# Operand layout and access order in the large fp32r matmuls of a two-block layer on one core

## The reference

```
h  = rmsnorm(concat(meta, x)) @ w_in          # 2048 x 10240, 272 rows
x  = x + merged(h) @ w_out
h  = rms_norm(x) @ w_in_2                     # retention, gated delta rule, gates
x  = x + merged2(h) @ w_out_2
x  = x + cross_attention(rms_norm(x) @ w_xq, rms_norm(mem) @ w_xkv) @ w_xo
x  = x + square(relu(rms_norm(x) @ w_ff1)) @ w_ff2
out = rms_norm(x)
```

## Time and profile before

| | |
|---|---|
| median of 3 runs | 2828.58 us |
| the profiled execution | 2828.21 us |
| its span, first to last instruction | 2826.5 us |
| TensorE matmul busy | 2808.4 us (99%) |
| TensorE weight load busy | 2442.2 us (86%) |
| VectorE busy | 1931.8 us (68%) |
| ScalarE busy | 1351.7 us (48%) |
| HBM traffic over the span | 178 GB/s |

### The profile page before, as it was taken

The page is one execution under the profiler, slowest core; times in us unless marked ns, Lnnn a source line. Parts: engine busy times, 40 slices in busy tenths (PEclk is TensorE's granted clock), DMA queues, the critical chain, the costliest instruction groups (busy, mean ns, idle before and its releaser), DMA issues.

```text
span 2826.5 us, 38749 instructions
## 1 busy us (share of the span) xinstructions
PE 2808.4 (99%) x15872; PEld 2442.2 (86%) x15872; DVE 1931.8 (68%) x2513; ACT 1351.7 (48%) x1726; POOL 59.2 (2%) x102
## 2 busy tenths in 40 slices
PE   9999999999999999999999999999999999999998
PEld 8899888888888888888888888888888888888887
DVE  7645567778766658898988875556666656666556
ACT  5434654347334436555555543444345434444434
POOL 0000210000000000000000000000000000000000
PEclk9999999999999999999999999999999999999999
DMA  7444344565555544434343445544354454554453
GB/s 278 179 188 156 145 173 182 189 235 192 201 182 190 185 178 170 145 139 149 135 149 135 159 170 196 200 185 161 139 199 188 179 208 182 205 200 188 185 203 149
DMA packets 72849, 506.66 MB, mean 179 GB/s; under 512 B 8384, under 2 KB 8512, under 8 KB 12896
## 3 DMA queue, kind: packets, MB, share of 16 engines
q1 hardware_dynamic: 71136, 497.83, 47.6%
q0 software_dynamic: 1104, 5.90, 0.6%
q10 hardware_dynamic: 432, 0.45, 0.0%
HBM read 499.95 MB, written 2.10 MB: 178 GB/s over the span
## 4 chain that ended last, share of the span: by engine, by line
PE 92%; DVE 5%; ACT 1%; issue 1%; DMA 1%; SPq 0%; POOL 0%; DVEq 0%; ACTq 0%
PE double L1376 85%; PE bank L1376 6%; DVE wlo L2079 1%; DVE cacc L2085 1%; PE bank L1379 1%; DVE cst L2102 0%; ACT whi L1737 0%; DVE AA L2085 0%; DVE cst L2079 0%; DMA vec<-in_vec 0%; DVE cacc L2082 0%; DVE Cm L2079 0%; DVE Tn L2593 0%; DMA raw<-in_wall 0%; DVE acc L2079 0%
## 5 line engine op out<-in xcount | busy, mean ns | idle before, releaser
L1376 PE MATMUL double<-AA,whi 128*128 128x512 f32 (+1 forms) x5008 | 1641.8, 380 | 2.8 <-DVE wlo L2079 2.8
L1737 ACT ACTIVATE whi<-raw 128x1024 fp32r<-128x1024 f32 x926 | 925.4, 1049 | 819.9 <-PE double L1376 780.7
L1376 PE MATMUL double<-AA,wlo 128*128 128x256 f32 (+1 forms) x4624 | 1296.4, 280 | 0.0
L2079 DVE TENSOR_TENSOR wlo<-raw,whi 128x1024 fp32r<-128x1024 f32 (+1 forms) x934 | 1101.1, 1214 | 195.0 <-ACT whi L1737 192.4
L1376 PEld LDWEIGHTS double<-AA,whi 128*128 128x128 f32 x5008 | 915.2, 188 | 180.5 <-DVE wlo L2079 4.6
L1376 PEld LDWEIGHTS double<-AA,wlo 128*128 128x128 f32 x4624 | 874.0, 189 | 1.4
L1376 PE MATMUL double<-whi,AA 128*128 128x512 f32 x1536 | 482.7, 389 | 0.7 <-DVE wlo L2079 0.7
L1376 PEld LDWEIGHTS double<-whi,AA 128*128 128x128 f32 x1536 | 288.5, 188 | 56.4 <-DVE wlo L2079 1.1
L1376 PE MATMUL double<-whi,BB 128*128 128x512 f32 x1024 | 309.1, 381 | 0.0
L1376 PE MATMUL double<-wlo,AA 128*128 128x512 f32 x768 | 296.5, 386 | 0.0
L1376 PEld LDWEIGHTS double<-whi,BB 128*128 128x128 f32 x1024 | 191.9, 187 | 33.7
(11 more groups left out here) (338 smaller groups left out, 1721.6 us busy)
## 6 DMA issues: line engine op xcount, KB each, us to landing
raw<-in_wall SPq DMA_DIRECT2D x462, 1024.0 KB, 4.8
raw<-in_wall SPq DMA_DIRECT2D x9, 256.0 KB, 6.4
X<-in_xT SPq DMA_DIRECT2D x1, 2048.0 KB, 11.3
Mm<-in_memT POOLq DMA_DIRECT2D x1, 2048.0 KB, 15.4
tmp<-rqk POOLq DMA_DIRECT2D x16, 128.0 KB, 2.2
mblk<-in_memT SPq DMA_DIRECT2D x8, 256.0 KB, 3.3
dec<-in_dec POOLq DMA_DIRECT2D x1, 1536.0 KB, 8.6
hs<-in_hsT SPq DMA_DIRECT2D x4, 272.0 KB, 5.6
```

The costliest lines, as they stand in the source:

```text
L1376: return q.matmul(out, lhsT, rhs, start=start, stop=stop, skip_group_check=True)
L1737: q.activation(hi_of(j)[:, c], raw[j % RAW][:, c], ACT.Copy).then_inc(S("w_hi"), 1)
L2079: return q.tensor_tensor(out, a, b, o)
```

## The change: what it does

The high and the low part of one k-tile now lie side by side: `AA` is seen as `[16, 2, 272]` (`AL`) or `[16, 2, 256]` (`AT`), `BB` as `[8, 2, 256]`. With the 256-wide layout `both` is one contiguous run of 512 columns. Kind T matmuls whose tag is not in `META_TAGS` walk moving operand and output by `leap` (4 rounds of runs of 8 with a step of 32, as kind N), over 512 columns and over 256; those in `META_TAGS` keep the plain order. `whi` and `wlo` have 32 and 48 spare columns, and `hi_of` and `lo_of` choose an offset so that every set begins at byte 128 of 256. The ScalarE and VectorE steps that write the parts follow the layout: those that wrote 512 contiguous columns (`A2`, `b_hi`, `b_lo`) write two runs of 256 with a gap of 256.

```diff
+META_TAGS = ("gp", "q", "mp", "ga", "ma")
...
-    whi = [ar.get([P_, UNIT + 0], F32R, f"whi{i}") for i in range(SPL)]
-    wlo = [ar.get([P_, UNIT + 64], F32R, f"wlo{i}") for i in range(SPL)]
+    whi_at = [ar.off + 4 * (UNIT + 32) * i for i in range(SPL)]
+    wlo_at = [ar.off + 4 * (UNIT + 32) * SPL + 4 * (UNIT + 48) * i for i in range(SPL)]
+    whi = [ar.get([P_, UNIT + 32], F32R, f"whi{i}") for i in range(SPL)]
+    wlo = [ar.get([P_, UNIT + 48], F32R, f"wlo{i}") for i in range(SPL)]
...
-    AA = ar.get([P_, 2, NT * L], F32R, "AA")
-    Ahi, Alo = AA[:, 0, :], AA[:, 1, :]
+    AA = ar.get([P_, 2 * NT * L], F32R, "AA")
+    AL = AA[:, :].rearrange("p (k s n) -> p k s n", s=2, n=L)
+    AT = AA[:, 0:2 * NT * T].rearrange("p (k s n) -> p k s n", s=2, n=T)
...
-    BB = ar.get([P_, 2, 8 * T], F32R, "BB")
+    BB = ar.get([P_, 8, 2, T], F32R, "BB")
...
     def A2(t, j):
-        return t[:, 2 * j * T:2 * (j + 1) * T]
+        return AT[:, 2 * j:2 * j + 2, t, :]
...
-        return (0, 16 if pr["kind"] == "T" else 0)
+        return (128, 128) if kind == "T" else (128, 128)
...
-        o = set_off(j)[0]
+        o = (set_off(j)[0] - whi_at[j % SPL]) % 256 // 4
...
-        o = set_off(j)[1]
+        o = (set_off(j)[1] - wlo_at[j % SPL]) % 256 // 4
...
             if pr["ready"][0] == "b_lo":
-                return BB[:, :, a * T:(a + 1) * T]
+                return BB[:, a, :, :]
             if pr["kind"] == "W":
-                o, n = a * L, L
-            elif pr["tag"] in ("gp", "q", "mp", "ga", "ma"):
-                o, n = a * L + META, T
-            else:
-                o, n = a * T, T
-            return AA[:, :, o:o + n]
-
-        def leap(x):
-            return x.rearrange("p (b s r) -> p s b r", s=4, r=8)
+                return AL[:, a, :, :]
+            if pr["tag"] in META_TAGS:
+                return AL[:, a, :, META:L]
+            return AT[:, a, :, :]
+
+        def leap(x, s=4, r=8):
+            return x.rearrange("p (b s r) -> p s b r", s=s, r=r)
...
-                        mm_group(out[0:n, m * 512:m * 512 + 2 * T], wh[:, i, c], both, start=first, stop=False)
-                        ins = mm_group(out[0:n, m * 512:m * 512 + T], wl[:, i, c], hh, start=False, stop=last)
+                        o, h = out[0:n, m * 512:m * 512 + 2 * T], out[0:n, m * 512:m * 512 + T]
+                        if pr["tag"] in META_TAGS:
+                            mm_group(o, wh[:, i, c], both, start=first, stop=False)
+                            ins = mm_group(h, wl[:, i, c], hh, start=False, stop=last)
+                        else:
+                            mm_group(leap(o, 4, 8), wh[:, i, c], leap(flat(both), 4, 8), start=first, stop=False)
+                            ins = mm_group(leap(h, 4, 8), wl[:, i, c], leap(hh, 4, 8), start=False, stop=last)
...
         def b_hi(i, r):
-            q.activation(flat(Bhi[:, 2 * i:2 * i + 2, :]), tmps[r["t"]][:, :], ACT.Copy).then_inc(S("b_hi"), 1)
+            q.activation(BB[:, 2 * i:2 * i + 2, 0, :], two(tmps[r["t"]][:, :]), ACT.Copy).then_inc(S("b_hi"), 1)
```

More of the change, by code:

```diff
@@ L1155, in program @@
     boff = ar.off
-    BB = ar.get([P_, 2, 8 * T], F32R, "BB")
-    Bhi = BB[:, 0, :].rearrange("p (a b) -> p a b", a=8)
-    Blo = BB[:, 1, :].rearrange("p (a b) -> p a b", a=8)
+    BB = ar.get([P_, 8, 2, T], F32R, "BB")
     q0 = ar.off
@@ L1337, in set_off @@
     def set_off(j):
-        pr = P.pairs[units[j][0]]
-        return (0, 16 if pr["kind"] == "T" else 0)
+        kind = P.pairs[units[j][0]]["kind"]
+        return (128, 128) if kind == "T" else (128, 128)
     def hi_of(j):
-        o = set_off(j)[0]
+        o = (set_off(j)[0] - whi_at[j % SPL]) % 256 // 4
         return whi[j % SPL][:, o:o + UNIT]
     def lo_of(j):
-        o = set_off(j)[1]
+        o = (set_off(j)[1] - wlo_at[j % SPL]) % 256 // 4
         return wlo[j % SPL][:, o:o + UNIT]
@@ L1761, in s_a1 @@
                 q.wait_ge(S(f"hs{HS[k]}"), 16)
-            q.activation(Ahi[:, k * L:(k + 1) * L], hs[:, k, :], ACT.Copy, scale=V("norm_gain", k)).then_inc(S("a_hi"), 1)
+            q.activation(AL[:, k, 0, :], hs[:, k, :], ACT.Copy, scale=V("norm_gain", k)).then_inc(S("a_hi"), 1)
         def s_sq0(j, r):
@@ L1827, in s_a2 @@
             q.wait_ge(S("merged"), at["au", k]["m"])
-            q.activation(A2(Ahi, k), flat(Macc[:, 2 * k:2 * k + 2, :]), ACT.Copy).then_inc(S("a_hi"), 1)
+            q.activation(A2(0, k), Macc[:, 2 * k:2 * k + 2, :], ACT.Copy).then_inc(S("a_hi"), 1)
         def s_nrm(key, r):
@@ L1877, in f @@
                 q.wait_ge(S("ev"), at["res", (r["res"], k // 2)]["ev"])
-                q.activation(Ahi[:, k * T:(k + 1) * T], X[:, k, :], ACT.Copy, scale=scale(k)).then_inc(S("a_hi"), 1)
+                q.activation(AT[:, k, 0, :], X[:, k, :], ACT.Copy, scale=scale(k)).then_inc(S("a_hi"), 1)
             return f
@@ L1980, in s_memn @@
             q.wait_ge(S("w_used"), r["used"])
-            q.activation(Ahi[:, k * T:(k + 1) * T], mblk[k // 2][:, k % 2 * T:(k % 2 + 1) * T], ACT.Copy,
+            q.activation(AT[:, k, 0, :], mblk[k // 2][:, k % 2 * T:(k % 2 + 1) * T], ACT.Copy,
                          scale=V("norm_mem_g_2", k)).then_inc(S("a_hi"), 1)
@@ L1998, in s_a4 @@
             q.wait_ge(S("w_used"), r["used"])
-            q.activation(A2(Ahi, j), flat(Macc2[:, 2 * j:2 * j + 2, :]), ACT.Copy).then_inc(S("a_hi"), 1)
+            q.activation(A2(0, j), Macc2[:, 2 * j:2 * j + 2, :], ACT.Copy).then_inc(S("a_hi"), 1)
         def s_x_s(h, r):
@@ L2011, in s_a6 @@
             q.wait_ge(S("xat_vec"), at["x_o", (j // 2, j % 2)]["o"])
-            q.activation(A2(Ahi, j), flat(Mx[:, 2 * j:2 * j + 2, :]), ACT.Copy).then_inc(S("a_hi"), 1)
+            q.activation(A2(0, j), Mx[:, 2 * j:2 * j + 2, :], ACT.Copy).then_inc(S("a_hi"), 1)
         def s_f1(i, r):
@@ L2118, in s_a1 @@
             q.wait_ge(S("a_hi"), r["hi"])
-            c = slice(k * L, (k + 1) * L)
-            stt(Alo[:, c], hs[:, k, :], V("norm_gain", k), Ahi[:, c].bitcast(F32), ALU.mult, ALU.subtract).then_inc(S("a_lo"), 1)
+            stt(AL[:, k, 1, :], hs[:, k, :], V("norm_gain", k), AL[:, k, 0, :].bitcast(F32), ALU.mult, ALU.subtract).then_inc(S("a_lo"), 1)
         def s_sq0(j, r):
@@ L2183, in b_lo @@
             q.wait_ge(S("b_hi"), r["hi"])
-            hi = flat(Bhi[:, 2 * i:2 * i + 2, :]).bitcast(F32)
-            tt(flat(Blo[:, 2 * i:2 * i + 2, :]), tmps[r["t"]][:, :], hi, ALU.subtract).then_inc(S("b_lo"), 1)
+            hi = BB[:, 2 * i:2 * i + 2, 0, :].bitcast(F32)
+            tt(BB[:, 2 * i:2 * i + 2, 1, :], two(tmps[r["t"]][:, :]), hi, ALU.subtract).then_inc(S("b_lo"), 1)
         def s_mix(g, r):
@@ L2278, in f @@
                 q.wait_ge(S("a_hi"), r["hi"])
-                tt(A2(Alo, j), src(j), A2(Ahi, j).bitcast(F32), ALU.subtract).then_inc(S("a_lo"), 1)
+                tt(A2(1, j), src(j), A2(0, j).bitcast(F32), ALU.subtract).then_inc(S("a_lo"), 1)
             return f
@@ L2284, in f @@
                 q.wait_ge(S("a_hi"), r["hi"])
-                c = slice(k * T, (k + 1) * T)
-                stt(Alo[:, c], X[:, k, :], gain(k), Ahi[:, c].bitcast(F32), ALU.mult, ALU.subtract).then_inc(S("a_lo"), 1)
+                stt(AT[:, k, 1, :], X[:, k, :], gain(k), AT[:, k, 0, :].bitcast(F32), ALU.mult, ALU.subtract).then_inc(S("a_lo"), 1)
             return f
@@ L2690, in s_memn @@
             q.wait_ge(S("a_hi"), r["hi"])
-            c = slice(k * T, (k + 1) * T)
-            stt(Alo[:, c], mblk[k // 2][:, k % 2 * T:(k % 2 + 1) * T], V("norm_mem_g_2", k), Ahi[:, c].bitcast(F32),
+            stt(AT[:, k, 1, :], mblk[k // 2][:, k % 2 * T:(k % 2 + 1) * T], V("norm_mem_g_2", k), AT[:, k, 0, :].bitcast(F32),
                 ALU.mult, ALU.subtract).then_inc(S("a_lo"), 1)
@@ L2799, in vector_program @@
                "k": s_k, "v": s_v, "vtr": s_vtr, "att_z": s_att_z, "att_o": s_att_o, "mp": gate_in(rx), "ma": gate_in(rx), "pu": s_pu,
-               "ga": s_ga, "au": s_au, "a2": split_low(lambda j: flat(Macc[:, 2 * j:2 * j + 2, :])),
+               "ga": s_ga, "au": s_au, "a2": split_low(lambda j: Macc[:, 2 * j:2 * j + 2, :]),
                "a3": gained_low(lambda k: g12[:, k:k + 1]), "a5": gained_low(lambda k: V("norm_x_g_2", k)),
-               "a7": gained_low(lambda k: V("norm_ffn_g_2", k)), "a4": split_low(lambda j: flat(Macc2[:, 2 * j:2 * j + 2, :])),
-               "a6": split_low(lambda j: flat(Mx[:, 2 * j:2 * j + 2, :])), "begin2": s_begin2, "res": s_res, "nrm": s_nrm,
+               "a7": gained_low(lambda k: V("norm_ffn_g_2", k)), "a4": split_low(lambda j: Macc2[:, 2 * j:2 * j + 2, :]),
+               "a6": split_low(lambda j: Mx[:, 2 * j:2 * j + 2, :]), "begin2": s_begin2, "res": s_res, "nrm": s_nrm,
                "fold": s_fold, "fin": s_fin, "mixs": s_mixs, "mixf": s_mixf, "xn": s_xn, "trig": s_trig, "gab": s_gab, "gab1": s_gab1,
```

## The result

The changed kernel takes 2835.13 us (median of 12 runs, 2834.31 to 2836.98) against 2828.65 us: a ratio of 1.0023 with a 95% interval of 1.0015 to 1.0031. It is 6.5 us slower, where 39 us less were forecast. The profiled execution has a span of 2833.3 us.

The account below looks back on a forecast made before the run. TensorE's matmul rate was taken as the bound. Kind T gains of 29.4 us (undisturbed stages) and 9.5 us (stages cut by side groups), other terms 0, gave 2828.2 - 38.9 = 2789 us; range 2763 to 2829.

Parts of the forecast that it names:

- What bounds the kernel: Whole kernel: TensorE matmuls busy 2808.4 of 2826.5 us, never kept waiting; the rate at which matmuls follow each other decides.
- the 10 that were named as the limit: Sign in the profile after: TensorE's waits should stay under 10 us in all.
- The 512 of a pair has f2's form ... I take 220 ns.: Kind T's 512-column matmul in runs of eight: from about 230 to 220 ns, bounds 220 and 230.
- The 256 measured 113, as taken: Kind T's 256-column matmul in runs of eight: 113 ns, half way between 109 and 117, because its load nearly fills it.
- Side groups leave the two streams in a new position ... I take half: pu, rq, rk, dq, dk, dv, xq, cut by side groups: half the gain, 1,408 pairs x 6.75 = 9.5 us.
- mk was counted as undisturbed: mk listed with au, wo, wo2, xo, f1 as uncut stages: 2,176 pairs at full gain, 29.4 us.
- mv and f2 are good already: Kind N stages mv and f2: already at the fast rate, no change counted.
- dealt anew: Kind N in rv, rg, gta, gz, gtb: states redistributed; all good gains 10.6 us, all bad costs as much; taken 0.
- I take 0: Changed start bytes in 896 plain pairs (-3 or +7 us) and kind W (2 us either way): 0 for both.
- no change (1): Rival: kind T stays at 230 + 117; time 2828, or 2825 to 2835 with the plain pairs; chance 0.11.
- The limit of 0.2%: Whole kernel time: within 0.2% (5.7 us) no measurement of this kernel can tell a change.
- Rival 4: Kind T slower: the 256 in runs of eight makes load and stream meet, pair about 358 ns, 2867 us; chance 0.12.

Follow-up runs that it names:

- Run 11: Changed kernel, but the second matmul of a kind T pair also moves all 512 columns, in the same runs; 3204.14 us, one run.
- run 4: Changed kernel, but only the 512-column matmul of a kind T pair in runs of eight, the 256 in plain order; 2846.64 us, ratio 1.0063.
- run 10: run 9's kernel, but kind T's 256-column matmul walked in two rounds of 128 columns (step 16) instead of four of 64; 2821.32 us, 0.9975.
- run 6: Kernel before the change, with only kind T's low weights moved from byte 192 to byte 128; 2851.97 us, ratio 1.0085.
- run 9: Changed kernel, but the kind T unit right before each kind N stage in plain order with low weights at byte 192; 2812.52 us, ratio 0.9944.
- run 5: Changed kernel, but kind T's low weights begin at byte 192 as in the kernel before; 2837.48 us, ratio 1.0044.

## Why the prediction was wrong

**What bounds the kernel** held: 99% busy, no wait of weight (11.6 us in all, a little over the 10 that were named as the limit), all in the rate at which matmuls follow each other; and that the run order has two rates, 220 and 231.

**"The 512 of a pair has f2's form ... I take 220 ns."** This term was mis-sized: it measured 227 (226 to 227). The form of a matmul is not enough, its neighbours belong to it. Run 11 shows 220 in f1 for the same operands with a second 512, run 4 shows 230 beside a plain 256. The 256 measured 113, as taken; that the weight load sets it was not tested. The pair is 340 and not 333, the term 22 us and not 39.

**"Side groups leave the two streams in a new position ... I take half"** was wrong for kind T, in the change's favour: after a side group the pairs of dk, dq and dv come back to 227 + 113 (means 226.9 and 114.3 against 226.7 and 113.5 in f1). In the changed kernel the pair has one steady rhythm, where kind N has two. With other edits the pair has more than one as well: in run 10 it took 341 in f1 and 352 in wo. And mk was counted as undisturbed, though 124 side matmuls cut into its stage; at half the gain that would have been 1.7 us less.

**"mv and f2 are good already"** is the step that failed, and it decided the sign. I saw that the rate of kind N is inherited, and applied that to the retention stages ("dealt anew"), with 10.6 us either way. I did not apply it to mv and f2, which ran at 220 throughout, though each follows a kind T stage that the change alters. They measured 230.6. Their 220 was a product of the old handover (runs 6 and 9); 20 us hung on it. With it in the range, 2829 would have been 2849.

**"I take 0" for the start bytes** was right for plain pairs and kind W (1.3 us together), and wrong in what it looked at: the byte of kind T's low weights was priced in the matmuls that read it, and it acts on f2, which doesn't read it (run 6). On those that read it, it acts as well once they go in runs: 340 a pair at byte 128, 350 at byte 192 (run 5).

**The rivals**: no change (1) reaches up to 2835 and so has the measured time, by luck: its mechanism, a kind T that gains nothing, is refuted by the 340. The range, which ended at 2829, left that upper part out without a reason. The limit of 0.2% below which no change could be told was too wide as well: the interval of the result is 1.0015 to 1.0031. Rival 4, slower by a bad 256, is refuted: the 256 gained. The rule of the Trainium skill in PSUM — Partial Sum Buffer, section Specifications (TRN2), that non-contiguous patterns slow matmuls, is contradicted for 256 columns too: 113 in runs of eight, 117 plain. The rule of the Trainium skill in SBUF — State Buffer, section Who interferes with whom, that TensorE never waits on anyone, is about one engine holding up another. It neither explains nor rules out what is seen here, the same f2 at 220 or at 230.6, since no run shows what f2 waits for; rival 1 read more out of it than it says.

**What stays open**: what the streams meet in. That it is their relative timing is an inference from two rates of one instruction stream; no run shows the collision itself. Nor is it known why mv and f2 took different rates in runs 5, 6 and 11, after kind T with the same bytes, or why the first f2 of run 4 differs from the others. Byte 192 with plain order gave 220 in both every time it was run; byte 128 mostly gave 230.6 or more, not always.

## What to carry to other kernels

A matmul rate that takes two values for one form belongs to the sequence, not to the instruction: before changing what stands ahead of a stage at the better rate, ask what put it there, and put its loss into the range. When a gain at one place and a loss at another come from the same constant, set it by place: here a single plain unit with another start byte before each stage turned 6.5 us lost into 16 us gained. And a form tested in one neighbourhood (512 after 512) is a bound for another (512 beside 256), not its price.

## What the runs showed of the hardware

With a mean granted clock of 0.998 to 0.999 in every run, an fp32r matmul of 512 columns with its own weight load took 220, 227, 230.6 or 232.8 ns in steady state (means over a stage), of 213.3 ns of streaming at 2.4 GHz, depending on the order in which columns are walked, on the start bytes of both operands and on what ran before. In f2 and mv the rate is kept for a whole stage: in f2 it lasted 192 matmuls, through unit boundaries and changes of the PSUM buffer. A start byte changed by 64 in weights used earlier moved a later stage by 5% (run 6). A matmul's recorded duration tells the rate at a glance: 380 to 382 ns at 220, 391 at 230.6.
